# The shared SBUF region of a retention and GLA block begins on a multiple of 64 bytes instead of 32

## The chip, the cores and the metric

One NeuronCore of a Trainium2 chip. The metric is the device time of one execution in microseconds (us). Float32 in and out; the large matrix products run in the type fp32r, each as three matmuls on a high and a low part.

## What is computed

`x` and `ctx_in` are 256 x 2048 (latent and context tokens). Cut to what matters:

```python
h  = rms_norm(x, norm_mix_pre) * (1 + sc1) + sh1
hc = rms_norm(ctx, norm_mix_pre) * (1 + scc) + shc
p  = h @ w_in                      # 11296 columns
pc = hc @ w_in[:, :N_CTX_COLS]     # the first 3616 of them
# retention and gated linear attention, 4 heads each, both directions, from p and pc
y_ret = o_r @ w_up_ret
y_gla = o_g @ w_up_gla
merged = sigmoid(gate_a) * y_ret + sigmoid(gate_b) * y_gla
h_state = h_state + g1 * rms_norm(merged @ w_out, norm_mix_post)
h = rms_norm(h_state, norm_ffn_pre) * (1 + sc2) + sh2
y = (silu(h @ ffn_w_gate) * (h @ ffn_w_up)) @ ffn_w_down     # 5632 inner columns
h_state = h_state + g2 * rms_norm(y, norm_ffn_post)
```

`sc1`, `sh1` and the like come from `silu(c) @ w_mod`, a 2048 x 12288 matrix.

## The kernel before

Every large product streams its weight matrix once. The weights are the moving operand, the activations the stationary one. SyncE loads a piece of 2 x 128 rows by 512 columns (512 KB) into the ring `raw` of eight slots; ScalarE's `split` (L595) writes its fp32r rounding to `w_hi`, a ring of four; VectorE's `split` (L912) writes the rest, `raw - w_hi`, to `w_lo`; TensorE's `products` (L1286 to L1288) then runs, for each of the two rows of blocks and each token tile,

```python
pe.matmul(o, hi[:, kk, c], w_hi[:, q, e, :], start=kk == 0, stop=False)
pe.matmul(o, hi[:, kk, c], w_lo[:, q, e, :], start=False, stop=False)
last = pe.matmul(o, lo[:, kk, c], w_hi[:, q, e, :], start=False, stop=kk == last_k)
```

The first tensor argument is the output in PSUM, the second the stationary tile (128 x 128), the third the moving one (128 x 512). One piece of the ring, a slot, is 2 x 2 x 3 = 12 matmuls where only the 256 latent tokens are multiplied, and 24 where the context tokens are too.

The order of the work, as TensorE sees it:

1. The opening: `silu(c) @ w_mod` for the first modulation, on a stationary tile of four columns (`c4`), with the eight slots of context block 0 in between.
2. Context blocks 1 to 6 (`ctx_block`), 48 slots of 24 matmuls, stationary `h_hi`, `h_lo`, `hc_hi`, `hc_lo`. Beside them ScalarE's queue loads `w_mod`'s further columns into `wm` (1 MB each) and VectorE multiplies and adds them (`add_chunk`, L924).
3. The gate projection (L1364, L1365): moving `h_hi`, `h_lo`, `hc_hi` and `hc_lo` in 256 columns, stationary `ga_hl` in 64.
4. Latent blocks, stationary `h_hi`, `h_lo`; the scans of the four heads are worked in between in plain float32.
5. Branch projections (`up_block`), 4 blocks of 8 slots, stationary `o_hi`, `o_lo`.
6. `w_out`, 4 blocks of 8 slots, then FFN gate and up, 11 blocks of 16 slots, stationary `h_hi`, `h_lo` again (rewritten).
7. FFN down, 4 blocks of 22 slots, stationary `hid_hi`, `hid_lo`.

SBUF is laid out by hand. `keep` places a tile for the whole run and rounds its size up to 32 bytes; after the last of them `base` is read from the cursor, and `reg` places the tiles of a shared region of 93 KB at `base` plus whole kilobytes, so that stages reuse each other's space. The byte addresses in a partition come out as follows:

| tiles | address before | past a multiple of 64 | past a multiple of 128 |
|---|---|---|---|
| `raw`, `w_hi`, `w_lo` | 16512, 49280, 65664 | 0 | 0 |
| `h_hi`, `h_lo` (also `xn`, `y2`, `hs2`) | 82048, 98432 | 0 | 0 |
| `base`, `o_hi`, `hid_hi`, `hs` | 133920 | 32 | 32 |
| `o_lo` | 150304 | 32 | 32 |
| `hc_hi`, `hc_lo` | 166688, 183072 | 32 | 32 |
| `hid_lo` | 178976 | 32 | 32 |
| `wm` | 199456 | 32 | 32 |
| `ga_hl`, `diag0` | 217888 | 32 | 32 |

The slices that a matmul takes of `w_hi`, `w_lo`, `h`, `hc`, `o` and `hid` are 512 or 2048 bytes long and follow each other without a gap, so each begins at the same place in 128 bytes as its tile.

Of the kernel before, what the change touches and what calls it, by code (L numbers as in the profile page):

```python
# [88 lines left out]
def build(nc, x, c, ctx_in, c_ctx, w_mod, b_mod, norm_mix_pre, norm_mix_post, norm_ffn_pre, norm_ffn_post,  # L89
# [10 lines left out]
    with ExitStack() as ctx:  # L100
        cursor = [(nc.sbuf_base + 31) // 32 * 32]
# [4 lines left out]
        def keep(name, shape, dt=F32):  # L106

            size = math.prod(shape[1:]) * (4 if dt != mybir.dt.uint8 else 1)
            off = cursor[0]
            cursor[0] += (size + 31) // 32 * 32  # L110
            return at(name, shape, dt, off)
# [40 lines left out]
        stats = keep("stats", [P, 2, MT, 6])  # L152
        mv = keep("mv", [P, 2, MT, 2])
        hr = keep("hr", [P, 2, MT, 1])
        base = cursor[0]
        K = 1024

        def reg(name, shape, kb, dt=F32):
# [1507 lines left out]
```

## Time and profile before

| | |
|---|---|
| median of three runs | 1865.39 us (1864.79, 1865.39, 1868.99) |
| profiled execution, from first to last instruction (its span) | 1862.4 us |
| mean granted TensorE clock | 0.983 of full speed |
| TensorE busy | 1795.3 us, 96% |
| VectorE, ScalarE, GpSimd busy | 1043.3, 788.0, 195.2 us |
| moved by DMA | 422.15 MB, 227 GB/s over the span |

The profile gives only the span of its own execution, no time around it; the nearest run stands 2.4 us above the span, the median 3.0 us. Matmuls are pipelined and their ends are modelled, so a TensorE that is always busy is not yet one at its peak: for the rate at which matmuls pass, their starts are read. Lines of the timeline are start in us, duration in us, engine, line of the kernel, operation, output and inputs by name (of a matmul the moving tile first, then the stationary one; for a high or low tile the last name tells which), shapes. The clock is in parts of full speed.

### The profile page before, as it was taken

How to read it: one execution, taken by the hardware profiler on the slowest of the kernel's cores; microseconds unless marked ns; L12 is line 12 of the kernel's file. 1: busy time of each engine (PE TensorE's matmuls, PEld its weight loads, DVE VectorE, ACT ScalarE, POOL GpSimd, SP SyncE). 2: the span in 40 equal slices, each digit the busy share in tenths (PEclk: the TensorE clock that was granted, in tenths of full speed). 3: DMA queues.
4: the chain of work that ended last, by engine and by line, in shares of the span. 5: the costliest groups of instructions: out<-in, count | busy, mean ns of one | idle time of the engine just before them, and what ended most of it. 6: DMA issues, size and time to landing. Idle time of an engine off the chain costs nothing.

```text
span 1862.4 us, 22224 instructions
## 1 busy us (share of the span) xinstructions
PE 1795.3 (96%) x8076; PEld 1445.3 (78%) x8076; DVE 1043.3 (56%) x1061; ACT 788.0 (42%) x861; POOL 195.2 (10%) x210
## 2 busy tenths in 40 slices
PE   4888999999999899999999999999999999999997
PEld 3446888888778787787888898888888888888885
DVE  3766666554765667766665445444544444444444
ACT  5654222222645444444544445444444444343442
POOL 1453000000006522430000000000000000000000
PEclk9999999999999999999999989999999999999999
DMA  8878998886988755654767745666666666766552
GB/s 307 274 255 284 330 333 304 304 313 235 323 309 304 261 175 168 197 180 128 230 222 283 243 147 175 189 190 190 181 189 192 190 187 190 256 187 188 190 186 76
DMA packets 182286, 422.15 MB, mean 227 GB/s; under 512 B 12817, under 2 KB 13121, under 8 KB 171601
## 3 DMA queue, kind: packets, MB, share of 16 engines
q1 hardware_dynamic: 156576, 304.25, 51.9%
q10 hardware_dynamic: 17568, 82.32, 12.1%
q0 software_dynamic: 8080, 34.75, 5.5%
q8 instruction: 40, 0.66, 0.1%
q14 instruction: 22, 0.17, 0.0%
HBM read 397.66 MB, written 23.61 MB: 226 GB/s over the span
## 4 chain that ended last, share of the span: by engine, by line
PE 89%; DVE 3%; ACT 2%; issue 2%; POOL 1%; DMA 1%; SPq 0%; DVEq 0%; ACTq 0%; POOLq 0%
PE ps L1286 26%; PE ps L1288 26%; PE ps L1287 26%; PE ps L1321 2%; ACT w_hi L595 1%; PE ps L1406 1%; PE ps L1470 1%; DVE w_lo L912 1%; POOL xr_t L364 1%; PE ps L1338 1%; PE ps L1499 1%; PE ps L1515 1%; PE ps L1553 1%; DMA xn<-in_ctx_in 1%; PE ps L1596 1%
## 5 line engine op out<-in xcount | busy, mean ns | idle before, releaser
L912 DVE TENSOR_TENSOR w_lo<-raw,w_hi 128x1024 fp32r<-128x1024 f32 x568 | 699.3, 1240 | 591.6 <-ACT w_hi L595 591.5
L595 ACT ACTIVATE w_hi<-raw 128x1024 fp32r<-128x1024 f32 x568 | 596.3, 1058 | 871.9 <-PE ps L1288 825.1
L1286 PE MATMUL ps<-w_hi,h_hi 128*128 128x512 f32 x1536 | 612.2, 399 | 6.8 <-POOL hc_lo L371 5.1
L1288 PE MATMUL ps<-w_hi,h_lo 128*128 128x512 f32 x1536 | 601.7, 392 | 0.0
L1287 PE MATMUL ps<-w_lo,h_hi 128*128 128x512 f32 x1536 | 601.2, 391 | 0.0
L1286 PEld LDWEIGHTS ps<-w_hi,h_hi 128*128 128x128 f32 x1536 | 290.0, 189 | 71.4 <-POOL hc_lo L371 5.7
L1288 PEld LDWEIGHTS ps<-w_hi,h_lo 128*128 128x128 f32 x1536 | 289.9, 189 | 62.4
L1287 PEld LDWEIGHTS ps<-w_lo,h_hi 128*128 128x128 f32 x1536 | 290.3, 189 | 59.7 <-issue 1.0
L924 DVE SCALAR_TENSOR_TENSOR acc<-wm,csil,acc 128x2048 f32<-128x2048 f32 (+1 forms) x60 | 141.0, 2350 | 99.5 <-DMA wm<-in_w_mod 99.4
L1288 PE MATMUL ps<-w_hi,hid_lo 128*128 128x512 f32 x352 | 140.4, 399 | 0.0
L1287 PE MATMUL ps<-w_lo,hid_hi 128*128 128x512 f32 x352 | 138.8, 394 | 0.0
L1286 PE MATMUL ps<-w_hi,hid_hi 128*128 128x512 f32 x352 | 138.1, 392 | 0.0
L1286 PE MATMUL ps<-w_hi,hc_hi 128*128 128x512 f32 x224 | 90.1, 402 | 0.0
L1287 PE MATMUL ps<-w_lo,hc_hi 128*128 128x512 f32 x224 | 89.8, 401 | 0.0
L1288 PE MATMUL ps<-w_hi,hc_lo 128*128 128x512 f32 x224 | 88.5, 395 | 0.0
L1287 PEld LDWEIGHTS ps<-w_lo,hid_hi 128*128 128x128 f32 x352 | 66.1, 188 | 17.2
L1286 PEld LDWEIGHTS ps<-w_hi,hid_hi 128*128 128x128 f32 x352 | 66.1, 188 | 15.6
L1288 PEld LDWEIGHTS ps<-w_hi,hid_lo 128*128 128x128 f32 x352 | 66.1, 188 | 15.3
L1321 PE MATMUL ps<-w_hi,c 128*4 128x512 f32 x128 | 52.4, 409 | 26.4 <-DVE w_lo L912 25.9
L1321 PE MATMUL ps<-w_lo,c 128*4 128x512 f32 x128 | 52.0, 406 | 0.0
L1321 PEld LDWEIGHTS ps<-w_hi,c 128*4 128x4 f32 x128 | 11.0, 86 | 51.8 <-DVE w_lo L912 21.7
L1286 PEld LDWEIGHTS ps<-w_hi,hc_hi 128*128 128x128 f32 x224 | 42.9, 191 | 10.5
(257 smaller groups left out, 1330.5 us busy)
## 6 DMA issues: line engine op xcount, KB each, us to landing
raw<-in_w_in SPq DMA_DIRECT2D x176, 512.0 KB, 5.5
wm<-in_w_mod ACTq DMA_DIRECT2D x64, 1024.0 KB, 6.9
raw<-in_ffn_w_gate SPq DMA_DIRECT2D x88, 512.0 KB, 4.1
raw<-in_ffn_w_up SPq DMA_DIRECT2D x88, 512.0 KB, 3.8
raw<-in_ffn_w_down SPq DMA_DIRECT2D x88, 512.0 KB, 4.6
raw<-in_w_mod SPq DMA_DIRECT2D x64, 512.0 KB, 5.4
raw<-in_w_out SPq DMA_DIRECT2D x32, 512.0 KB, 5.0
px<-stage ACTq DMA_DIRECT2D x44, 256.0 KB, 6.5
```

The costliest lines, as they stand in the source:

```text
L364: last = eng.tensor_scalar(t, t, scale1[:, e, k:k + 1], mod_t[:, k, e:e + 1], ALU.mult, ALU.add)
L595: act.activation(w_hi[:, j % SPLIT, :, :], raw[:, j % RAW, :, :], ACT.Copy).then_inc(w_high, 1)
L912: dve.tensor_tensor(w_lo[:, j % SPLIT, :, :], raw[:, j % RAW, :, :], w_hi[:, j % SPLIT, :, :].bitcast(F32), ALU.subtract).then_inc(w_low, 1)
L924: dve.scalar_tensor_tensor(out=a, in0=wm[:, b, :], scalar=csil[:, k:k + 1], in1=a, op0=ALU.mult, op1=ALU.add).then_inc(S("wm_used"), 1)
L1286: pe.matmul(o, hi[:, kk, c], w_hi[:, q, e, :], start=kk == 0, stop=False)
L1287: pe.matmul(o, hi[:, kk, c], w_lo[:, q, e, :], start=False, stop=False)
L1288: last = pe.matmul(o, lo[:, kk, c], w_hi[:, q, e, :], start=False, stop=kk == last_k)
L1321: last = pe.matmul(bank(4 + n % 2)[0:4, :], c4[:, :, k], w[:, s % SPLIT, e, :], start=k == 0 and w is w_hi, stop=k == KT - 1 and w is w_lo)
L1338: last = pe.matmul(bank(k % 4)[:, m * P:(m + 1) * P], xn[:, m, k * P:(k + 1) * P], diag0[:, m, :], start=True, stop=True)
L1406: last = pe.matmul(dst[:, first + k:first + k + 1], sums[:, g, k * P:(k + 1) * P], ones[:, :], start=True, stop=True)
L1470: last = pe.matmul(bank(6, 2)[:, e * L + m * P:e * L + (m + 1) * P], g_arg[:, 1, e, key * P:(key + 1) * P], g_arg[:, 0, e, qry * P:(qry + ...
L1499: last = pe.matmul(bank(4, 2)[:, a * L:(a + 1) * L], r_kt[:, 2 * (a // 2) + f, (a % 2) * P:(a % 2 + 1) * P], r_qt[:, f, :], start=f == 0, ...
```

## The change

`base` is rounded up to the next multiple of 64. Every tile that `reg` places moves by the same 32 bytes, from 133920 to 133952 and so on: all of them are then on a multiple of 64, and 64 past one of 128. Tiles placed by `keep`, and those at fixed places in the space of `h` and `stage`, stay. The instructions of each engine and their order are the same.

```diff
         stats = keep("stats", [P, 2, MT, 6])
         mv = keep("mv", [P, 2, MT, 2])
         hr = keep("hr", [P, 2, MT, 1])
-        base = cursor[0]
+        base = (cursor[0] + 63) // 64 * 64
         K = 1024
 
         def reg(name, shape, kb, dt=F32):
```

## Rows read from the trace of the kernel before

**Rows 1.** The page's head, busy time by engine, and granted clock in 40 slices.
```profile
span 1862.4 us, 22224 instructions
...
PE 1795.3 (96%) x8076; PEld 1445.3 (78%) x8076; DVE 1043.3 (56%) x1061; ACT 788.0 (42%) x861; POOL 195.2 (10%) x210
...
PEclk9999999999999999999999989999999999999999
```

**Rows 2.** The page's chain of waits, share of the span by engine and line.
```profile
PE 89%; DVE 3%; ACT 2%; issue 2%; POOL 1%; DMA 1%; SPq 0%; DVEq 0%; ACTq 0%; POOLq 0%
PE ps L1286 26%; PE ps L1288 26%; PE ps L1287 26%; PE ps L1321 2%; ACT w_hi L595 1%; PE ps L1406 1%; PE ps L1470 1%; DVE w_lo L912 1%; POOL xr_t L364 1%; PE ps L1338 1%; PE ps L1499 1%; PE ps L1515 1%; PE ps L1553 1%; DMA xn<-in_ctx_in 1%; PE ps L1596 1%
```

**Rows 3.** Timeline of PE in the FFN's gate and up blocks.
```profile
1235.03 0.39 PE L1286 MATMUL ps<-w_hi,h_hi 128*128 128x512 f32 x1
1235.26 0.39 PE L1287 MATMUL ps<-w_lo,h_hi 128*128 128x512 f32 x1
...
1237.75 0.39 PE L1286 MATMUL ps<-w_hi,h_hi 128*128 128x512 f32 x1
```

**Rows 4.** Timeline of PE in the down projection.
```profile
1700.16 0.39 PE L1286 MATMUL ps<-w_hi,hid_hi 128*128 128x512 f32 x1
1700.39 0.39 PE L1287 MATMUL ps<-w_lo,hid_hi 128*128 128x512 f32 x1
...
1702.96 0.39 PE L1286 MATMUL ps<-w_hi,hid_hi 128*128 128x512 f32 x1
```

**Rows 5.** Timeline of PE in the branch projections.
```profile
949.70 0.39 PE L1286 MATMUL ps<-w_hi,o_hi 128*128 128x512 f32 x1
...
952.50 0.39 PE L1286 MATMUL ps<-w_hi,o_hi 128*128 128x512 f32 x1
```

**Rows 6.** Windows: stretch, its us, busy us (instructions), clock, DMA share, GB/s.
```profile
205.00:305.00 100.00, 100.00 (x434) 81.07 (x433) 65.48 (x40) 23.68 (x27) 0.00 (x0) 1.00 0.91 329
...
1230.00:1330.00 100.00, 100.00 (x450) 82.93 (x450) 48.72 (x41) 42.03 (x41) 0.00 (x0) 1.00 0.65 189
...
1640.00:1740.00 100.00, 100.00 (x430) 80.47 (x429) 45.55 (x38) 40.69 (x44) 0.00 (x0) 1.00 0.61 187
```

**Rows 7.** Matmuls on `hid`: duration min/median/max in ns, first and last start.
```profile
L1286 PE MATMUL ps<-w_hi,hid_hi x352: 392/392/482, 1603.4 to 1850.0; 128*128 128x512 f32 x176
L1288 PE MATMUL ps<-w_hi,hid_lo x352: 392/399/399, 1603.8 to 1850.4; 128*128 128x512 f32 x176
```

**Rows 8.** Timeline of PE in the context blocks, 24 matmuls from first to last.
```profile
298.45 0.40 PE L1286 MATMUL ps<-w_hi,h_hi 128*128 128x512 f32 x1
...
304.01 0.40 PE L1286 MATMUL ps<-w_hi,h_hi 128*128 128x512 f32 x1
```

**Rows 9.** Timeline of PE in the gate projection and the first matmul behind it.
```profile
448.57 0.28 PE L1364 MATMUL ps<-h_hi,ga_hl 128*64 128x256 f32 x1
...
452.36 0.28 PE L1364 MATMUL ps<-hc_hi,ga_hl 128*64 128x256 f32 x1
...
456.00 0.40 PE L1286 MATMUL ps<-w_hi,h_hi 128*128 128x512 f32 x1
```

**Rows 10.** Waits from 1605 to 1850 us: total us, times, longest.
```profile
ACT w_hi L595 <- PE ps L1288: 139.7, 83, 2.0
DVE w_lo L912 <- ACT w_hi L595: 126.7, 84, 1.9
```

**Rows 11.** Timeline, float32 matmuls on `xn` and `hs` in merged runs.
```profile
37.77 1.95 PE L1338 MATMUL ps<-diag,xn 128*128 128x128 f32 x16
...
1113.42 1.05 PE L1596 MATMUL ps<-diag,hs 128*128 128x128 f32 x8
```

**Rows 12.** Waits from 190 to 440 us, and VectorE's two operations of a slot.
```profile
ACT w_hi L595 <- PE ps L1288: 154.4, 38, 4.6
DVE acc L924 <- DMA wm<-in_w_mod: 88.7, 41, 4.9
...
217.35 2.35 DVE L924 SCALAR_TENSOR_TENSOR acc<-wm,csil,acc 128x2048 f32 x1 [1.02 <-DMA wm<-in_w_mod]
219.62 1.22 DVE L912 TENSOR_TENSOR w_lo<-raw,w_hi 128x1024 fp32r<-128x1024 f32 x1
```

## The prediction

> **What bounds the kernel now.** I read the views in the order of the groups ahead. The page's first part shows TensorE busy for 1795.3 of 1862.4 us, with every other engine at 56% or less, and the granted clock at its full level in nearly every slice [rows 1]. The chain of waits, followed back from the last instruction, is 89% TensorE, and 78 points of it are the three matmul lines of `products` [rows 2]. So this kernel is a long row of 128x128 by 128x512 matmuls, and what counts is the **pitch**, the time from the start of one to the start of the next. The durations on the page (some 392 to 402 ns) overlap and are modelled, so I leave them aside and take starts.
>
> The pitch is not the same in all stages. In the FFN's gate and up blocks, where the stationary tile is `h_hi` or `h_lo`, twelve matmuls, one slot of the weight ring, go from 1235.03 to 1237.75 us: 2.72 us, 226.7 ns each [rows 3]. In the down projection, where it is `hid_hi` or `hid_lo`, twelve go from 1700.16 to 1702.96: 2.80 us, 233.3 ns each [rows 4]. In the branch projections (`o_hi`, `o_lo`) it is 949.70 to 952.50, again 2.80 us [rows 5]. The moving tiles `w_hi` and `w_lo`, the clock and the form of the instruction are the same in all three; in every one the engine has a next matmul at hand, for a stretch of 100 us is busy to 100.00 at clock 1.00 [rows 6]. That it holds for the whole down stage: 1056 matmuls of `hid` start between 1603.4 and 1850.4 us [rows 7]; 247.0 us less some 0.9 us for eight small transposes in between, over 1055 steps, is 233.3 ns.
>
> What differs is the address. `w_hi`, `w_lo`, `h_hi` and `h_lo` all begin at a multiple of 128 bytes; every tile of the region begins at one of 64 plus 32. The context stage mixes both: of 24 matmuls in a slot twelve have `h` and twelve `hc` as the stationary tile. Twenty-four go from 298.45 to 304.01 us, 5.56 us [rows 8], against 5.44 for two slots of `h` alone. So 0.12 us more where half of them are off by 32.
>
> One place lets me tell the address from the part of memory. In the gate projection at 448 us the stationary tile is `ga_hl` of the region. With `h` as the moving tile, 32 matmuls go from 448.57 to 452.36, 118.4 ns each; with `hc`, itself in the region, 32 go from 452.36 to 456.00, 113.8 ns each [rows 9]. There it is the region's tile pair that is quick. So a stationary tile 32 bytes past a multiple of 64 is not slow by itself. What fits both places is the offset of the two operands **against each other**: zero (both on a multiple of 64, or both 32 past one) is quick, 32 is slow. This is my reading of two places, not something that the trace names.
>
> **The change part by part.** It adds 32 bytes to `base`, from 133920 (2092 times 64, plus 32) to 133952. No instruction, wait, transfer or order changes; the only effect can be in how long things take. The region's tiles move as one, so two operands that both lie in it keep their offset.
>
> 1. *Down projection.* 4 column blocks of 22 slots are 88 slots, each 2.80 us now and 2.72 if `hid` behaves as `h`: 88 x 0.08 = **7.0 us**. The stage is on the path throughout: ACT's split waits 139.7 us for matmuls to free a ring slot there and waits for no load at all [rows 10].
> 2. *Branch projections.* 4 blocks of 8 slots: 32 x 0.08 = **2.6 us**.
> 3. *Context blocks 1 to 6.* 48 slots of 24 matmuls: 48 x (5.56 - 5.44) = **5.8 us**. Here a transfer might come first, see the second case below.
> 4. *Context block 0*, eight slots spread through the opening, where TensorE often waits on others. At least nothing, at most 8 x 0.12 = 1.0 us. Its last two slots run on into block 1 with no wait behind them, so I take 2 x 0.12 = **0.2 us**.
> 5. *The gate projection*: 32 matmuls with moving `h`, 118.4 to 113.8 ns, 0.15 us at most; I count zero.
> 6. *Float32 matmuls of the heads, sums and transposes.* Nothing. Most have both operands in the region. And they show no effect of the offset: with stationary `xn` (a multiple of 64) against `diag0` (32 past one), 16 take 1.95 us; with `hs` and `diag` both in the region, 8 take 1.05 us [rows 11]. The eight more cost 0.90 us, 112 ns each, the same pitch that seven steps and the tail of the second give, so equal and unequal offsets cost the same there. Bounds of this term: 0.5 us either way.
> 7. *Vector, scalar and GpSimd work and transfers on region tiles.* Zero. TensorE covers it: ACT spends 139.7 and 154.4 us waiting for it in the two long stages [rows 10, 12], and a change of some ns per instruction does not use that up. At the very end, behind the last matmul, some 10 us are uncovered, but their large tiles `y2` and `hs2` lie in the `h` space and do not move. If that cover went, 3.6 us of VectorE work per context slot (2.35 and 1.22 us) would have to pass the slot's 5.4 us.
>
> Sum: 7.0 + 2.6 + 5.8 + 0.2 = **15.6 us**. The sum is made against the profiled span of 1862.4 us, which would become 1846.8. The median of the runs shown is 3.0 us above that span (start and end around it, and other executions), which the change does not touch: 1865.4 - 15.6 = **1849.8 us**, 0.84% faster.
>
> What speaks against it: a stationary tile's address should not matter to the moving stream. The Trainium skill ("TensorE: Matmul & The Clock Gate", Step-by-step: what each phase is for) gives the engine two independent read ports, one for the streaming operand and one for LDWEIGHTS, and its page "SBUF — State Buffer" (Specifications) puts the cache line at 16 bytes, of which 32 and 64 are both multiples. By these two the change would bring nothing; the 2.72 and 2.80 us of the rows say that some property of the tiles matters all the same.
>
> **The rivals.**
>
> *Only part comes.* In the context stage the transfers keep the queues 91% busy at 329 GB/s, and VectorE waits 88.7 us for `wm` in its 250 us [rows 6, 12]. If that stream cannot run faster, slots there stay at 5.56 us and terms 3 and 4 drop: 1865.4 - 9.6 = 1855.8 us. For it: these numbers. Against it: a slot asks for 1.57 MB of loads (512 and 1024 KB) and 0.13 MB of stores, which in 5.44 us is 313 GB/s, below the 329 that was moved; and no wait for a `raw` load shows. Other partial results (a smaller but not zero cost at an offset of 64) lie at the same place.
>
> *No change.* The slow pitch belongs to something else that sets `hid`, `o` and `hc` apart: that they lie beyond 131072 bytes while the moving tiles lie below, or that the offset must vanish in 128 bytes rather than 64. After the change the region is 64 past a multiple of 128, and `w_hi` is on one. `ga_hl` against `hc` and `h` fits that too: same side quick, other side slow. Then the time stays at 1865.4 us. Against the first: a split of the memory would be expected to help two operands on different sides. Against the second, nothing in the trace; no tile now stands 64 from its partner in the products. The skill's 16-byte line, as a mechanism of this kernel, is this case as well, since the shift would cross no line differently.
>
> *Slower.* The pattern repeats in 128 bytes or more and an offset of 64 is its worst point. Place: every product with a region tile, 1056 + 384 + 672 = 2112 matmuls. Price: if the excess doubles, terms 1 to 4 turn round, and the time is 1865.4 + 15.6 = 1881.0 us. It decides as soon as the pitch in the down stage passes 235 ns, since 1.8 ns on 2112 matmuls are 3.7 us. For it, only that 64 is untried; against it, that the small offset already costs and the trace has no case where more distance costs more.
>
> That the change does nothing to the address is excluded: 133920 is no multiple of 64.
>
> **How the numbers follow.** Forecast 0.73, part only 0.10, no change 0.10, slower 0.07. A measurement of this kernel can tell about 0.2% (3.7 us) from no change. The first two are faster by more than that, 0.83; no change 0.10; slower 0.07. The predicted time is the likeliest case's, 1849.8. The range goes below it by the bounds of terms 4 to 6 (0.8, 0.15 and 0.5 us) and the spread of a median, to 1847.5, and above it past the partial case to 1861, where a third of the gain is left; the last two cases stay outside, 0.17 together.
>
> **What would show it.** Right: the down and branch stages at 2.72 us for twelve matmuls, the context stage at 5.44 us for twenty-four, the FFN's gate and up stage unchanged at 2.72, float32 groups unchanged, and 32 matmuls with moving `h` in the gate projection at some 114 ns. Wrong as a whole: 2.80 us in the down stage. Wrong in a term: 2.72 there but 5.56 in the context stage with ACT or VectorE waiting for loads. If `ga_hl` with moving `h` stays at 118 ns while the products become quick, it is the stationary tile's own address that counts and not the offset between the two.

## The result, and the profile after

The changed kernel takes 1854.28 us (median of six runs, 1849.09 to 1860.49) against 1865.09 us for the kernel before (six runs, 1863.49 to 1868.99). The ratio is 0.9942, with a 95% interval from 0.9929 to 0.9954: 0.6% faster, 10.8 us. A second set of runs of the same kernel gave 1854.67 us, ratio 0.9942 (0.9928 to 0.9955). The forecast was 15.6 us and 1849.8 us; the direction and the place were right, the size was 1.4 times what came. One run on record stands apart: an execution of the kernel whose region is 96 past a multiple of 128 took 2578.25 us at a mean granted clock of 0.653, and is left out of that kernel's median below.

The page of the changed kernel, its head and busy times, against [rows 1]:

```profile
span 1852.6 us, 22224 instructions
...
PE 1784.2 (96%) x8076; PEld 1446.4 (78%) x8076; DVE 1043.3 (56%) x1061; ACT 787.5 (43%) x861; POOL 196.0 (11%) x210
```

The span fell by 9.8 us and TensorE's busy time by 11.1; VectorE and ScalarE do what they did. Now the pitch, from the timeline of PE, in the order of [rows 3, 4, 5, 8]: the FFN's gate and up blocks, the down projection, the branch projections (twelve matmuls each), the context stage (twenty-four).

```profile
1234.72 0.39 PE L1286 MATMUL ps<-w_hi,h_hi 128*128 128x512 f32 x1
...
1237.44 0.39 PE L1286 MATMUL ps<-w_hi,h_hi 128*128 128x512 f32 x1
...
1700.11 0.39 PE L1286 MATMUL ps<-w_hi,hid_hi 128*128 128x512 f32 x1
1700.34 0.39 PE L1287 MATMUL ps<-w_lo,hid_hi 128*128 128x512 f32 x1
...
1702.86 0.39 PE L1286 MATMUL ps<-w_hi,hid_hi 128*128 128x512 f32 x1
...
950.22 0.39 PE L1286 MATMUL ps<-w_hi,o_hi 128*128 128x512 f32 x1
...
952.97 0.39 PE L1286 MATMUL ps<-w_hi,o_hi 128*128 128x512 f32 x1
...
298.00 0.39 PE L1286 MATMUL ps<-w_hi,h_hi 128*128 128x512 f32 x1
...
303.46 0.39 PE L1286 MATMUL ps<-w_hi,h_hi 128*128 128x512 f32 x1
```

On `h` a slot still takes 2.72 us. On `hid` and `o` it takes 2.75 us: less than the 2.80 of before, but more than the 2.72 of the forecast. The context slot takes 5.46 us instead of 5.56, where 5.44 was forecast. Over the whole down stage (1598.3 to 1840.6 us, first and last start):

```profile
L1286 PE MATMUL ps<-w_hi,hid_hi x352: 392/394/475, 1598.3 to 1840.2; 128*128 128x512 f32 x176
L1288 PE MATMUL ps<-w_hi,hid_lo x352: 388/392/397, 1598.8 to 1840.6; 128*128 128x512 f32 x176
```

242.3 us less the 0.9 us of the eight transposes, over 1055 steps, is 228.8 ns against 233.3 [rows 7] and 226.7 on `h`. In what follows I give the time of a slot of twelve to the nanosecond; it is the median over the stage's slots, from the starts in the trace: 2.800 before, **2.747** after, 2.720 on `h`. The context slot's are 5.560, 5.467 and 5.440.

The gate projection, against [rows 9]:

```profile
442.86 0.28 PE L1364 MATMUL ps<-h_hi,ga_hl 128*64 128x256 f32 x1
...
446.60 0.28 PE L1364 MATMUL ps<-hc_hi,ga_hl 128*64 128x256 f32 x1
...
450.22 0.39 PE L1286 MATMUL ps<-w_hi,h_hi 128*128 128x512 f32 x1
```

With moving `h` 32 matmuls take 3.74 us, 116.9 ns each, down from 118.4; with moving `hc` 113.1 each. Here too the region's pair is the quick one, and the mixed pair has come closer without reaching it.

Where the time went, by the first starts: the gate projection begins at 442.86 instead of 448.57, 5.7 us earlier; the down stage at 1598.3 instead of 1603.4, 5.1 us; the last matmul starts at 1840.6 instead of 1850.4, 9.8 us. The first of these is 1.0 us more than the shorter slots up to there give (4.5 us in context blocks 1 to 6, some 0.2 in block 0). Some 0.4 us of it is there at the first matmul on `hc`, at 73.73 instead of 74.15 us; the rest was not traced. Between the first two points some 2.3 us are given back, for the branch projections, which lie there, became 1.7 us shorter. Two things are seen there: the granted clock from 1080 to 1130 us is 0.80 instead of 0.83, and TensorE waits for VectorE. From 540 to 600 us, where the last loads of `wm` meet those of `raw`, TensorE waited 0.2 us before and waits 1.7 us after (PE's waits in that stretch, of before and of after):

```profile
PE ps L1286 <- DVE w_lo L912: 0.2, 1, 0.2
```

```profile
PE ps L1286 <- DVE w_lo L912: 1.7, 1, 1.7
```

What held VectorE up there is the row of its `acc` in the timeline of the changed kernel, ahead of the `w_lo` in its queue; the bracket gives its own wait, 2.36 us for `wm`:

```profile
554.35 2.35 DVE L924 SCALAR_TENSOR_TENSOR acc<-wm,csil,acc 128x2048 f32<-128x2048 f32 x1 [2.36 <-DMA wm<-in_w_mod]
```

### The profile page after: what moved, and what is told of

Its sections match the earlier page's. It is cut to its first block, busy times and chain, and to the rows that moved or that the text cites. A ratio compares the mean times of both kernels' runs of the same rounds, so it can differ in the third digit from the quotient of the medians.

```text
span 1852.6 us, 22224 instructions
## 1 busy us (share of the span) xinstructions
PE 1784.2 (96%) x8076; PEld 1446.4 (78%) x8076; DVE 1043.3 (56%) x1061; ACT 787.5 (43%) x861; POOL 196.0 (11%) x210
## 4 chain that ended last, share of the span: by engine, by line
PE 90%; DVE 3%; ACT 2%; issue 2%; POOL 1%; DMA 1%; SPq 0%; DVEq 0%; ACTq 0%; POOLq 0%
PE ps L1286 27%; PE ps L1288 26%; PE ps L1287 26%; PE ps L1321 2%; PE ps L1406 1%; ACT w_hi L595 1%; PE ps L1470 1%; POOL xr_t L364 1%; DVE w_lo L912 1%; PE ps L1338 1%; PE ps L1499 1%; PE ps L1515 1%; PE ps L1553 1%; DMA xn<-in_ctx_in 1%; PE ps L1596 1%
## 5 line engine op out<-in xcount | busy, mean ns | idle before, releaser
L1288 PEld LDWEIGHTS ps<-w_hi,hid_lo 128*128 128x128 f32 x352 | 66.1, 188 | 15.4
L1286 PE MATMUL ps<-w_hi,o_hi 128*128 128x512 f32 x128 | 50.6, 395 | 0.0
```

## The experiments

The theory going in: the pitch depends on the offset between the moving and the stationary tile, and what is left is the price of an offset of 64. Of several kernels there is only one run. Whole times scatter by some us between executions of one kernel (1849.09 to 1860.49 for the changed one), so those kernels are judged by their slot times, which hardly do. All later diffs are against the changed kernel.

**The region on a multiple of 128.**

```diff
-        base = (cursor[0] + 63) // 64 * 64
+        base = (cursor[0] + 127) // 128 * 128
```

> The region begins on a multiple of 128. Theory: the pitch depends on the offset between moving and stationary tile within 128 bytes, and what is left after the change (twelve matmuls on hid 2.747 us against 2.720 on h) is the price of an offset of 64. Then twelve on hid and on o take 2.72, twenty-four in the context stage 5.44, and the time falls by a further 88 x 0.027 + 32 x 0.027 + 50 x 0.027 = 4.6 us, to some 1849.7 us. Rival, the remainder belongs to the place of the region in memory: 2.747 and 5.467 stay, 1854.3 us.

Measured: 1848.81 us (five runs, 1848.03 to 1852.52), ratio to the kernel before 0.9915 (0.9901 to 0.9929). The windows of this run, and then the same stretch of the down stage (1660 to 1760 us) in the kernel before and in the changed one, one fence each; columns are the stretch, its us, then busy us and instructions of PE, PEld (TensorE's loading of stationary tiles), DVE, ACT and POOL, the clock, DMA share and GB/s:

```profile
205.00:305.00 100.00, 100.00 (x443) 82.84 (x442) 67.24 (x40) 23.13 (x26) 0.00 (x0) 1.00 0.91 328
...
1660.00:1760.00 100.00, 100.00 (x443) 82.84 (x442) 47.37 (x39) 40.15 (x41) 0.00 (x0) 1.00 0.60 194
```

```profile
1660.00:1760.00 100.00, 100.00 (x430) 80.44 (x429) 45.54 (x39) 40.69 (x44) 0.00 (x0) 1.00 0.61 187
```

```profile
1660.00:1760.00 100.00, 100.00 (x438) 82.05 (x438) 46.56 (x39) 41.57 (x45) 0.00 (x0) 1.00 0.61 190
```

TensorE is busy to 100.00 and at full clock in all three, and yet passes 430, 438 or 443 matmuls in the 100 us: the busy column hides what the count tells. A slot takes 2.720 us on `hid` and on `o`, 5.440 in the context stage, and the gate projection's mixed pair falls to 113.6 ns. The rest of the gain came exactly where the theory put it; that the region's place in memory keeps the remainder is refuted, for it moved by only 64 bytes more. In the context stage 443 matmuls passed (434 before, [rows 6]), with the transfers at 328 GB/s, so they were no obstacle there.

**The changed kernel again, beside it on the same chip.**

> The changed kernel once more, beside the others on the same chip. Both theories: twelve matmuls on hid in 2.747 us, the time 10 to 12 us below the kernel before, near 1854 us.

Measured: 1854.67 us (five runs, 1852.27 to 1860.15). All slots as in the first profile, 2.747 and 5.467. Its profiled span is 1858.5 us, 5.9 us over the first one, and what could be traced of that lies mostly in the clock, not in the pitch: from 160 to 200 us the granted clock was 0.96 against 1.00, from 540 to 600 us 0.94 against 0.97. Windows of this run:

```profile
160.00:200.00 40.00, 39.28 (x168) 29.94 (x167) 28.91 (x32) 15.39 (x20) 3.08 (x4) 0.96 0.94 324
540.00:600.00 60.00, 57.66 (x258) 47.56 (x257) 33.28 (x25) 27.55 (x35) 24.71 (x18) 0.94 0.90 313
```

and of the first profile of the changed kernel:

```profile
160.00:200.00 40.00, 39.28 (x175) 31.26 (x175) 26.60 (x30) 14.33 (x19) 3.08 (x4) 1.00 0.95 334
540.00:600.00 60.00, 58.27 (x267) 48.23 (x266) 34.60 (x25) 29.79 (x37) 28.94 (x19) 0.97 0.91 317
```

In these two stretches 16 matmuls fewer passed, which at the pitch of 227 to 229 ns is some 3.7 us; 0.6 us of it is a longer wait for VectorE (2.3 us against 1.7). Another 1.3 us was there before the first matmul on `hc` (75.00 against 73.73 us). So a single span tells the gain of this change only to some us; the slot times tell it without that scatter.

**The region 96 past a multiple of 128.**

```diff
-        base = (cursor[0] + 63) // 64 * 64
+        base = (cursor[0] + 127) // 128 * 128 - 32
```

> The region begins 96 past a multiple of 128, so the offset to the moving tile is 96, or 32 the other way. If only the distance within a circle of 128 bytes counts: 2.80 us for twelve on hid, as at 32, and 1865 us. If the circle is longer or the direction counts: another value, between 2.72 and 2.80 if it lies between 64 and 128 (some 2.735, 1852 us).

Measured: 1865.18 us (nine runs, 1861.65 to 1866.08), ratio 0.9994 (0.9984 to 1.0003), no change from the kernel before. A slot on `hid` takes 2.800 us again, a context slot 5.573 (5.560 before). This odd multiple of 32 costs a slot on `hid` what the kernel before paid.

**Everything moved by 32, the offsets between the tiles zero.**

```diff
-        cursor = [(nc.sbuf_base + 31) // 32 * 32]
+        cursor = [(nc.sbuf_base + 31) // 32 * 32 + 32]
...
-        base = (cursor[0] + 63) // 64 * 64
+        base = (cursor[0] + 127) // 128 * 128 + 32
```

> Every tile, moving ones too, begins 32 past a multiple of 128. Offset theory: all offsets between the tiles are zero, so twelve matmuls take 2.72 us on h and on hid, and the time is that of the region on a multiple of 128, some 1850 us. Rival, the stationary tile's own address counts: twelve take 2.80 us on h as on hid, 384 slots of h cost 384 x 0.08 = 31 us more, and the time is some 1865 + 31 = 1896 us.

Measured: 1848.84 us (four runs, 1847.25 to 1850.43), ratio 0.9908 (0.9892 to 0.9923). The down stage and the FFN's gate and up stage in windows of this run:

```profile
1300.00:1400.00 100.00, 100.00 (x451) 82.97 (x450) 48.67 (x40) 42.78 (x41) 0.00 (x0) 1.00 0.66 193
1660.00:1760.00 100.00, 100.00 (x443) 82.84 (x442) 46.99 (x39) 40.51 (x42) 0.00 (x0) 1.00 0.61 193
```

No tile of the matmuls lies on a multiple of 64, and every slot is quick. This refutes the stationary tile's own address as the cause, and with it the wording of the change: "a multiple of 64" is not what counts. Nor did VectorE, ScalarE or the transfers need the alignment, as far as the time can tell: it is that of the region on a multiple of 128.

**Only `h` off by 32.** The region on a multiple of 128, and one line more. The tiles that `keep` places behind `h` move along; of the tiles in `products`, only `h` does.

```diff
+        cursor[0] += 32
         h_off = cursor[0]
```

> Only h moves to 32 past a multiple of 128; the moving tiles and the region are on one. Offset theory: the roles change, twelve matmuls on h take 2.80 us and on hid 2.72, some 384 x 0.08 = 31 us more than with all on a multiple of 128: 1880 us. Rival, the stage or the place in memory decides: h stays at 2.72.

Measured: 1875.21 us (one run, 1864.86 for the kernel before beside it). The roles change: the gate and up stage passes 439 matmuls in 100 us where the run with the region on a multiple of 128 had 451, the down stage 443. Windows:

```profile
1300.00:1400.00 100.00, 100.00 (x439) 80.77 (x438) 48.54 (x40) 41.01 (x40) 0.00 (x0) 1.00 0.64 184
1660.00:1760.00 100.00, 100.00 (x443) 82.81 (x442) 46.98 (x40) 41.75 (x45) 0.00 (x0) 1.00 0.61 193
```

A slot of `h` takes 2.800 us, one of `hid` 2.720. Against the run with the region on a multiple of 128 it is 26.4 us slower; 31 were expected for all 384 slots. Part of the difference went into TensorE's other waits: between 400 and 1000 us they sum to 17.8 us in the run with the region on a multiple of 128 and to 15.0 us here, 2.8 us of the 4.3 that are missing (384 x 0.08 is 30.7). The tile `h_hi` lies at byte 82080 both here and in the run with everything moved; with the moving tiles on a multiple of 128 a slot on it takes 2.800 us, with them 32 past one 2.720.

**`w_lo` and `h` off by 32.** The region on a multiple of 128, and:

```diff
+        cursor[0] += 32
         w_lo = keep("w_lo", [P, SPLIT, 2, N], F32R)
```

> w_lo and h are 32 past a multiple of 128, w_hi and the region are on one. The offset is then 32 for w_hi with h (two of three matmuls) and for w_lo with hid (one of three). If the price falls on the matmul that streams the unequal moving tile, twelve on h take about 2.72 + 0.053 = 2.773 us, twelve on hid 2.72 + 0.027 = 2.747, and on hid only the step that begins with the w_lo matmul is longer. Rival, both moving tiles must be unequal or one unequal pair spoils all: 2.80 or 2.72 on both.

Measured: 1886.3 us (one run). 2.800 us on `h` and 2.800 us on `hid`. On `hid` the one unequal pair is `w_lo` with `hid_hi`, and it costs as much as three unequal pairs do. So the price is not paid matmul by matmul. The rival wins here. The steps on `hid` are 232, 236 and 232 ns, the one from `w_lo` on being the longest, but all three are longer than 227.

**`hid_lo` alone moved**, the region on a multiple of 128. Four runs of this form, with 32, 64, 128 and 256 bytes in the place of 32. The small tiles `hid_n` and `junk2` behind it move along:

```diff
-            return at(name, shape, dt, base + kb * K)
+            return at(name, shape, dt, base + int(kb * K))
...
-        hid_lo = reg("hid_lo", [P, FF_BLOCKS * 4, L], 44, F32R)
-        hid_n = reg("hid_n", [P, MT, N], 88)
+        hid_lo = reg("hid_lo", [P, FF_BLOCKS * 4, L], 44 + 32 / K, F32R)
+        hid_n = reg("hid_n", [P, MT, N], 88 + 32 / K)
...
-        junk2 = reg("junk2", [P, N], 88)
+        junk2 = reg("junk2", [P, N], 88 + 32 / K)
```

> The region is on a multiple of 128, hid_lo alone 32 past it. hid_lo is the stationary tile of each third matmul and is loaded while the one before it, hid_hi with w_lo, streams. If loading the next stationary tile disturbs the moving stream, the step from hid_hi with w_lo to hid_lo with w_hi is longer and twelve take about 2.747 us. If the tile's address matters in its own matmul, the step from hid_lo with w_hi to the next is longer instead. Rival, no effect of a single tile: 2.72.

Measured with 32: 2.800 us for a slot, 1853.22 us (one run). The steps, from the timeline, with the load of `hid_lo` (PEld) between them:

```profile
1699.74 0.40 PE L1286 MATMUL ps<-w_hi,hid_hi 128*128 128x512 f32 x1
...
1699.97 0.40 PE L1287 MATMUL ps<-w_lo,hid_hi 128*128 128x512 f32 x1
1699.97 0.19 PEld L1288 LDWEIGHTS ps<-w_hi,hid_lo 128*128 128x128 f32 x1
...
1700.21 0.39 PE L1288 MATMUL ps<-w_hi,hid_lo 128*128 128x512 f32 x1
...
1700.44 0.40 PE L1286 MATMUL ps<-w_hi,hid_hi 128*128 128x512 f32 x1
```

To the nanosecond they are 232, 239 and 229. The longest is the one during which `hid_lo` is loaded, as the first theory of the expectation had it, but its sum of 2.747 us was wrong, for the other two steps are longer than 227 as well. At an offset of 32 one unequal tile costs as much as two.

> The region is on a multiple of 128, hid_lo alone 128 further, so that its offset is 0 within 128 bytes and 128 within 256. If the pattern repeats in 128 bytes: 2.72 us for twelve on hid, 1850 us. If in 256 or more: another value for the steps that concern hid_lo.

Measured with 128: 2.773 us, 1852.43 us (one run); steps of 227, 233 and 234 ns. An offset of 128 is not free, so the pattern does not repeat in 128 bytes. My table of addresses ahead of the prediction, which stops at 128, was too short.

> hid_lo alone 64 further. The changed kernel, both 64 away, had 2.747. If each round of three pays by its most distant tile: 2.747. If the unlike offsets of hid_hi and hid_lo cost on top: 2.773 or 2.80. If each tile paid for itself: 2.72 + 0.009 = 2.729.

Measured with 64: 2.773 us, 1853.63 us (one run); steps of 228, 229 and 236 ns. Here the longest step is the one behind the load of `hid_lo`, so which step pays is not the same at every offset, and the first theory does not hold in general.

> hid_lo alone 256 further. Period of 256 bytes: 2.720. Longer period: 2.747 to 2.80, with the steps that touch hid_lo longer than 227 ns.

Measured with 256: 2.720 us, 1850.27 us (one run). Windows of the down stage, with 128 and with 256:

```profile
1660.00:1760.00 100.00, 100.00 (x434) 81.84 (x434) 46.51 (x39) 39.49 (x40) 0.00 (x0) 1.00 0.61 190
```

```profile
1660.00:1760.00 100.00, 100.00 (x443) 82.81 (x442) 47.17 (x39) 40.49 (x41) 0.00 (x0) 1.00 0.62 193
```

**Both `hid` tiles moved.** The same edit with `hid_hi` at `0 + 128 / K` or `0 + 256 / K` too.

> Both hid tiles begin 128 bytes further than in the run with the region on a multiple of 128, so both are 128 from the moving tiles. If the pattern repeats in 128 bytes and only a difference between hid_hi and hid_lo made the run with hid_lo alone 128 further slow: 2.720 us for twelve. If it repeats in 256 or more: above 2.720, and by the run with hid_lo alone (2.773) between 2.73 and 2.80.

Measured with 128: 2.791 us in the median of the stage's slots (2.780 to 2.795 for most), 1857.06 us (one run).

> Both hid tiles 256 further. If the pattern repeats in 256 bytes: 2.720 us for twelve. If an offset of 256 still costs, the period is at least 512 (a slice of a stationary tile is 512 bytes long, and half the slices already lie 512 apart in the quick case, so 512 is the longest it can be).

Measured with 256: 2.720 us, 1854.65 us (one run). So 256 counts as zero, and 128 does not: the pattern repeats in 256 bytes, as far as the offsets tried can tell. The whole time is above the 1850.27 us of the run with `hid_lo` alone 256 further, though the slots are the same; its clock is 0.96 from 160 to 200 us and 0.94 from 540 to 600 us, as in the second profile of the changed kernel.

All that was measured of a slot in the down stage or, for the offset of 32, in the FFN's gate and up stage. The offset is the stationary tile's address less the moving one's, within 256 bytes (`w_hi` and `w_lo` lie 128 past a multiple of 256, except in the run with everything moved):

| offset of both stationary tiles | kernel | twelve matmuls, us |
|---|---|---|
| 0 | `h` in the kernel before; region on a multiple of 128; everything moved; `hid` by 256 | 2.720 |
| 32 | only `h` off by 32 | 2.800 |
| 128 | both `hid` by 128 | 2.791 |
| 160 | the kernel before | 2.800 |
| 192 | the changed kernel | 2.747 |
| 224 | region 96 past a multiple of 128 | 2.800 |

With `hid_hi` at 0 and `hid_lo` alone away: 2.800 at 32, 2.773 at 64 and at 128, 2.720 at 256. Two of my expectations speak of the changed kernel as 64 away; within 256 bytes it is 192 away, and an equal offset of 64 was not run. A multiple of 128 was not enough by itself either: `base` came out 128 past a multiple of 256, where `w_hi` and `w_lo` lie, and both `hid` tiles 128 further are also on a multiple of 128 and take 2.791.

## Why the prediction was right, and where its size was off

*What bounds the kernel.* Right. No instruction and no order changed, and the time followed the pitch. The prediction's "busy to 100.00" for 100 us in every stage is shown by [rows 6] for two of its three only; for the branch projections the trace has 60.00 of 60.00 us, from 920 to 980 us at clock 1.00.

*The offset between the two operands as the cause.* Shown by two runs: with everything on 32 past a multiple of 128 all stages are quick, and with `h` alone moved it is `h` that becomes slow, at the same address of `h`. The place in memory and the stationary tile's own address are refuted by the same two. The prediction's sentence that "zero (both on a multiple of 64, or both 32 past one) is quick, 32 is slow" named the right quantity in the wrong circle: it is 256 bytes long, not 64. That the change helped at all was partly luck. It moved the offset from 160 to 192, which costs 0.027 us a slot; had it come to 128, also a multiple of 64, the slot would have gone only from 2.800 to some 2.791.

*The step that failed* is the "if `hid` behaves as `h`" of term 1, carried through terms 2, 3 and 5: two tiles on multiples of 64 were counted as having no offset, and a third of the slot's price stayed. Term 1: 88 x (2.800 - 2.747) = 4.7 us in place of 7.0; the stage's own starts give 247.0 - 242.3 = 4.7. Term 2: 32 x 0.053 = 1.7 in place of 2.6. Term 3: 48 x (5.560 - 5.467) = 4.5 in place of 5.8. Term 4, by the same reading, 0.2. Together 11.1 us, against 10.8 between the medians and 9.8 between the two profiled spans. Against the spans two differences partly cancel, the 1.0 us more ahead of the gate projection and the 2.3 us given back behind it. With the offset at zero the slots take what the terms had summed, and the gain is 15.4 us between the spans (1862.4 and 1847.0), 16.8 between the medians.

*The rivals.* "Only part comes" is what happened, and by its second half, a smaller but not zero cost, which the prediction gave no working of its own. Its first half, transfers that hold the context stage back, is wrong for that stage, whose slots shortened, but came true in a small way behind it: from 540 to 600 us TensorE waits for a `w_lo` that stands behind a load, 1.7 us in the changed kernel, 2.3 in its second profile, 2.1 with the region on a multiple of 128 and 0.2 before. Whether the quicker slots bring this about was not tested. That its 1855.8 us lies nearer to the 1854.28 measured than the forecast does is chance: it was worked out by dropping the context stage's gain and keeping the down stage's whole one, and neither happened. "The offset must vanish in 128 bytes" was closer to the truth than the forecast's 64, though it is 256 and the price between is graded. The third, *slower*, by which an offset of 64 is the "worst point" of the pattern, did not happen; how well founded that worry was, the runs show: another step of 32 bytes, to 96 past a multiple of 128, takes the whole gain away again.

*The float32 matmuls.* Nothing came there, as expected. The ones that tell are those of `xn` against `diag0`, for their offset changed, counted in the same way, from 96 before to 64 in the changed kernel and to 0 with the region on a multiple of 128: sixteen take 1.95 us in all three. The eight on `hs`, with both operands in the region, take 1.05 us as before.

*The rules weighed in the prediction.* The prediction took the Trainium skill's 16-byte line ("SBUF — State Buffer", Specifications) and its two independent read ports ("TensorE: Matmul & The Clock Gate", Step-by-step) to mean that an offset such as these costs nothing. The rows have 2.720 to 2.800 us for the same twelve matmuls, so the measurement decides against that reading.

*Open.* Why the price is what it is. The slot times 2.720, 2.747, 2.773 and 2.800 us lie 0.027 us apart, which at the upper clock level of 2.4 GHz is, by this estimate, 64 cycles for twelve matmuls, 16 for each round of three; 2.791 (both `hid` tiles at 128) doesn't fall on this ladder. Nor does the price carry over to a context slot, where rounds on `h` and on `hc` alternate two by two. Its twelve matmuls on `hc` cost 0.120 us before, where twelve on `hid` cost 0.080; 0.133 with the region 96 past a multiple of 128; and 0.093 with `h` moved in their place. In the changed kernel it is 0.027 in both. Term 3 was right to take its price from the context slot itself. No run separates the possible causes.

## What to carry to other kernels

When matmuls stand back to back, read the pitch from their starts and compare it between stages with the same instruction form; here a difference of 3%, with TensorE at 100% busy and at full clock in both, came from where the operands lie. Lay fp32r tiles out so that the addresses of moving and stationary slices are equal within 256 bytes. It is not enough to round both to 64 or 128: place the one by the other. Here this gave 1848.8 us, 0.85% under the kernel before (ratio 0.9915), where rounding to 64 gave 0.6% and another 32 bytes nothing. If one remedy fits the good case (a multiple of 64), ask which longer period the good case also satisfies, and go to that at once if it is free.

## What was not expected

At odd multiples of 32, one unequal pair in a round of three costs the full price: with `hid_lo` alone off by 32 a slot takes 2.800 us, as it does on `h` with both stationary tiles off by 32. At 128 it is 0.053 us for `hid_lo` alone against 0.071 for both. And the price isn't monotonic in the distance: an offset of 192 costs 0.027 us a slot, its neighbours 160 and 224 cost 0.080, and 128 costs 0.071.
